# First norm of a two-layer diffusion backbone: the shift leaves the tile path, and six products get their bias from separate small matmuls

## What is computed

```python
def rmsnorm(x, g):
    y = xf * lax.rsqrt(jnp.mean(xf * xf, -1, keepdims=True) + NORM_EPS)
    return (y * g.astype(jnp.float32)).astype(x.dtype)

def modulate(h, g, shift, scale):
    return rmsnorm(h, g) * (1 + scale) + shift

def adaln_terms(s, w, b):
    return jnp.split(jax.nn.silu(s) @ w + b, N_MOD, -1)

def swiglu(x, w_up, w_down):
    gate, up = jnp.split(x @ w_up, 2, -1)
    return (jax.nn.silu(gate) * up) @ w_down
```

## Time and profile before

| | |
|---|---|
| three runs | 3075.9 us median (3070.89 to 3077.01) |
| span of the profiled execution | 3074.0 us |
| time before the fourth product, u1, starts on PE | 77.27 us |
| busy | PE 97%, DVE 52%, ACT 32%, POOL 32% |
| chain that ended last | PE 89%, of which the dense products 78% |

### The profile page before, as it was taken

The page is one execution under the profiler, slowest core; times in us unless marked ns, Lnnn a source line. Parts: engine busy times, 40 slices in busy tenths (PEclk is TensorE's granted clock), DMA queues, the critical chain, the costliest instruction groups (busy, mean ns, idle before and its releaser), DMA issues.

```text
span 3074.0 us, 45849 instructions
## 1 busy us (share of the span) xinstructions
PE 2973.5 (97%) x19023; PEld 2784.3 (91%) x19023; DVE 1600.5 (52%) x2437; ACT 983.4 (32%) x1700; POOL 996.1 (32%) x516
## 2 busy tenths in 40 slices
PE   6999999999999988999999999999999999999998
PEld 6999999999888876899999999999999877798997
DVE  6556666884646665576667783212123358431223
ACT  4211212343454456321121233212123247532222
POOL 5333333333332202233333332222222222344442
PEclk8999999999999999999999999999999999999999
DMA  4434444223320022234334331211211210132221
GB/s 190 141 114 135 122 141 138 89 85 120 115 68 15 8 87 77 89 112 149 126 130 142 121 117 64 69 56 63 68 61 50 81 42 2 63 101 92 90 96 70
DMA packets 126236, 284.25 MB, mean 92 GB/s; under 512 B 40222, under 2 KB 57550, under 8 KB 126030
## 3 DMA queue, kind: packets, MB, share of 16 engines
q1 hardware_dynamic: 123150, 274.86, 27.4%
q10 hardware_dynamic: 2880, 6.47, 0.5%
HBM read 269.68 MB, written 15.10 MB: 93 GB/s over the span
## 4 chain that ended last, share of the span: by engine, by line
PE 89%; DVE 5%; ACT 4%; issue 2%; POOL 0%; DMA 0%; ACTq 0%; SPq 0%; DVEq 0%; POOLq 0%
PE psum L1788 78%; PE psum L1962 2%; PE psum L2062 2%; PE psum L2050 1%; DVE o_acc L1618 1%; PE psum L2043 1%; PE psum L1947 1%; ACT prob_o L1269 1%; PE psum L2003 1%; DVE prob_o L1719 1%; PE psum L1982 1%; PE psum L1969 1%; PE psum L1992 0%; DVE probT_o L1731 0%; ACT cacc L1122 0%
## 5 line engine op out<-in xcount | busy, mean ns | idle before, releaser
L893 POOL TENSOR_TENSOR wl<-raw,wh 128x1024 fp32r<-128x1024 f32 (+1 forms) x329 | 838.2, 2548 | 1643.8 <-ACT wh L998 1642.6
L1788 PE MATMUL psum<-uh,wh 128*128 128x256 f32 (+5 forms) x2704 | 660.0, 325 | 24.7 <-DVE ul L1336 17.7
L1788 PE MATMUL psum<-ul,wh 128*128 128x256 f32 (+5 forms) x2704 | 658.6, 325 | 0.0
L1788 PE MATMUL psum<-uh,wl 128*128 128x256 f32 (+5 forms) x2704 | 658.5, 325 | 0.0
L1788 PE MATMUL psum<-ah,wh 128*128 128x386 f32 (+4 forms) x2192 | 596.4, 344 | 5.6 <-POOL wl L893 4.4
L1788 PE MATMUL psum<-ah,wl 128*128 128x386 f32 (+4 forms) x2192 | 591.3, 342 | 0.0
L1788 PE MATMUL psum<-al,wh 128*128 128x386 f32 (+4 forms) x2192 | 589.0, 341 | 0.0
L1788 PEld LDWEIGHTS psum<-uh,wh 128*128 128x128 f32 (+1 forms) x2704 | 450.7, 189 | 48.5 <-issue 21.5
L1540 DVE SCALAR_TENSOR_TENSOR ada_product<-ada_w,cb 128x1024 f32<-128x1024 f32 x256 | 478.1, 1868 | 5.1
L1788 PEld LDWEIGHTS psum<-uh,wl 128*128 128x128 f32 (+1 forms) x2704 | 450.6, 189 | 19.7
L1788 PEld LDWEIGHTS psum<-ul,wh 128*128 128x128 f32 (+1 forms) x2704 | 450.0, 189 | 19.8
(11 more groups left out here) (248 smaller groups left out, 2433.9 us busy)
## 6 DMA issues: line engine op xcount, KB each, us to landing
raw<-in_w SPq DMA_DIRECT2D x264, 512.0 KB, 3.6
ada_w<-in_ada_w SPq DMA_DIRECT2D x128, 512.0 KB, 3.6
raw<-in_w SPq DMA_DIRECT2D x64, 448.0 KB, 3.4
spill<-cacc ACTq DMA_DIRECT2D x16, 384.0 KB, 2.6
scale_w<-in_scale_w SPq DMA_DIRECT2D x8, 512.0 KB, 13.6
ada_start<-in_ada_w SPq DMA_DIRECT2D x8, 512.0 KB, 14.4
ada_w<-bias_final SPq DMA_DIRECT2D x16, 256.0 KB, 3.0
h<-in_xT SPq DMA_DIRECT2D x8, 384.0 KB, 13.8
```

The source lines that it names most:

```text
L893: nc.gpsimd.tensor_tensor(wl[n % SPLIT_SLOTS][:, 0:k * w], raw[n % RAW_SLOTS][:, 0:k * w], wh[n % SPLIT_SLOTS][:, 0:k * w].bitcast(f32), A ...
L1788: ins = nc.tensor.matmul(pair[0:w, lo:hi], wt[n % SPLIT_SLOTS][:, k * w:(k + 1) * w], xt[:, k, cols], start=first, stop=last)
```

## The change

- silu(c) is loaded as a row, broadcast by one DMA to all partitions (cb, 1 MB), and goes through SiLU on ACT (one 128x2048 instruction). The 16 spreading matmuls and the two copies are gone.
- The shift leaves the tile path: `start_scale`, gain, uh and ul stay per tile, all eight scales on PE (`PE_SCALES`). The 8 shift chunks, now two passes each, are made by DVE after the tiles: 2 chunks before the norm, 3 behind the scaling of the fused products, 3 behind that of u1.
- The first six products (`early`: g0, u0, g1, u1, g2, u2) run over 768 columns without the shift. A new item `bias` makes their biases: in the middle of u2 (k = 4, `BIAS_AT`) PE runs 6 x 8 x 2 = 96 matmuls of 4 or 2 moving columns over the weights of all six products, kept for that: the first three in buffers of their own (`start_wh`, `start_wl`), the next three in wh and wl, which so stay taken until then.
- Only then do SiLU and gating of these products run (ACT and DVE, behind `bias_copied`); DVE copies each bias into the two end columns.
- DVE makes the low parts of the first three weights and sums the squares; POOL has nothing to do in the start. Four of the eight shift chunks are loaded over the buffers of scales 0 to 3.
- In all norms the shift columns are written by one instruction per kind of token, not per tile.

```diff
+EARLY = 6
+PE_SCALES = (0, 1, 2, 3, 4, 5, 6, 7)
+CHUNKS_BEFORE_NORM, CHUNKS_BEFORE_FOURTH = 2, 5
+BIAS_AT = 4
...
+            load_start(2)
+            sp.dma_start(cb[:, :, :].rearrange("p v d -> p (v d)"), a["c_rows"].to_broadcast([P, 2 * D])).then_inc(c_rows_loaded, 16)
...
+            sp.wait_ge(start_gain, 4)
+            for k in range(4, KD):
+                load_ada_start(k)
...
-                    if n >= SPLIT_SLOTS:
-
-                        act.wait_ge(product_done, number[slots[n - SPLIT_SLOTS][0]] + 1)
...
+                    if n >= FUSED + SPLIT_SLOTS:
+                        y = slots[n - SPLIT_SLOTS][0]
+                        act.wait_ge(product_done, number[("bias",) if y in early[FUSED:-1] else y] + 1)
...
+                elif x[0] == "bias":
+                    act.wait_ge(start_shift, 1)
+                    for v in range(2):
+                        nc.scalar.activation(shift_x[:, :, 1 - v], mod[:, 0, 0, :, v], ACT.Copy)
+                    shift_high(0, uh)
+                    split_up_to(EARLY + 1)
+                    for y in early[:-1]:
+                        finish_product(y)
...
+                if x in early:
+                    nc.vector.tensor_tensor(t[:, 1:1 + T], bank[:, AT:AT + T], rstd[:, 1:1 + T], ALU.mult).then_inc(scaled, 1)
...
-                ada_chunk(ada_order[k])
+                for n in ((0,), (1, 2))[k] if k < 2 else ():
+                    low_split(n)
                 late_low(norm_items[0], k)
-                start_shifts(k)
-                dve.wait_ge(shift_hi, k + 1)
-                shift_low(0, k).then_inc(shift_lo, 1)
-            dve.wait_ge(c_rows_copied[1], 1)
+                if k:
+                    add_square(0, k - 1)
+            add_square(0, KD - 1)
+            for c in ada_order[:CHUNKS_BEFORE_NORM]:
+                ada_chunk(c)
...
+                elif x == early[FUSED]:
+                    scale_product(x)
+                    for c in ada_order[CHUNKS_BEFORE_FOURTH:ADA_FIRST]:
+                        ada_chunk(c)
+                    start_shifts()
...
+            def early_biases():
+
+                pe.wait_ge(scaled, scaled_no[early[FUSED]] + 1)
+                pe.wait_ge(shift_lo, 1)
+                for y in early:
+                    n, bank = slot_of[y], bias_columns(y)
+                    for k in range(KD):
+                        nc.tensor.matmul(bank, high_weight(n)[:, P * k:P * k + P], shift_x[:, k, :], start=k == 0, stop=False)
+                        ins = nc.tensor.matmul(bank[:, 0:2], low_weight(n)[:, P * k:P * k + P], shift_x[:, k, 0:2],
+                                               start=False, stop=k == KD - 1)
+                ins.then_inc(product_done, 1)
...
-                    pe.wait_ge(ident_loaded, 16)
-                    for v in range(2):
-                        for q in range(KD):
-                            ins = nc.tensor.matmul(c_rows(v)[:, P * q:P * q + P], c_cols[:, q, v:v + 1].to_broadcast([P, P]), ident[:, :],
-                                                   start=True, stop=True)
-                    ins.then_inc(c_rows_made, 1)
...
                         pe.wait_ge(late_lo, k + 1)
-                        pe.wait_ge(shift_lo, k + 1)
...
+                    if x == early[-1]:
+                        ready = lambda k: early_biases() if k == BIAS_AT else None
```

More of the change, by code:

```diff
@@ L72, in over @@
             plan.setdefault(chosen[len(chosen) * c // len(chunks)], []).append(chunk)
-    at = [i for i, x in enumerate(items) if x[0] in ("gate", "up", "down") and x[1:3] == (0, 0)][FUSED:]
+    at = [i for i, x in enumerate(items) if x[0] in ("gate", "up", "down") and x[1:3] == (0, 0)][EARLY - 1:]
     n = next(k for k, i in enumerate(at) if items[i][0] == "down")
@@ L84, in schedule @@
     late = lambda m, products, n=1: products[:n] + [("norm", m)] + products[n:]
-    s = [("start",)] + late(0, ffn_products(0, 0), FUSED)
+    s = insert_before([("start",)] + late(0, ffn_products(0, 0), FUSED), ffn_products(0, 0)[EARLY - 1], [("bias",)])
     if mixers:
@@ L235, in build @@
     late_proj = {l: [x for x in late_items if x[0] == "proj" and x[1] == l] for l in range(DEPTH)}
-    fused = ahead[0]
+    fused, early = ahead[0], [x for x in late_items if norm_of(x) == 0][:EARLY]
     with ExitStack() as ctx:
@@ L429, in released @@
                 return [(start_gain, KD)]
+            if kind == "bias":
+                return [(bias_copied, 2 * EARLY)]
             if kind in RESIDUAL:
@@ L475, in build @@
                 place[x] = (4, 1)
+            elif kind == "bias":
+                place[x] = (7, 1)
             elif kind in ("vt", "start"):
@@ L498, in start_bank, with bias_columns, high_weight, low_weight @@
         def start_bank(k):
-            return banks_of(("start",))[:, 512 * (k % 2):512 * (k % 2) + 2]
-        def c_rows(v):
-            return psum[:, D * v:D * v + D]
+            b = PE_SCALES.index(k) % 2
+            return banks_of(("start",))[:, 512 * b:512 * b + 2]
+        def bias_columns(x):
+            return banks_of(("bias",))[:, 4 * early.index(x):4 * early.index(x) + 4]
+        def high_weight(n):
+            return start_wh[n] if n < FUSED else wh[n % SPLIT_SLOTS]
+        def low_weight(n):
+            return start_wl[n] if n < FUSED else wl[n % SPLIT_SLOTS]
         def segs_of(x):
@@ L1059, in late_high @@
                     act.wait_ge(mod_ready, mod_terms(x, 0, 1))
-                    for k in range(KD):
-                        ins = shift_high(m, k, high)
-                    ins.then_inc(shift_hi, 1)
+                    shift_high(m, high)
                 for v, (lo, hi) in enumerate((LAT, CTX)):
@@ L1536, in ada_chunk @@
                     w, product = ada_w[n % ADA_BUFS], ada_product
-                for v in range(2 if n >= ADA_FIRST else 1):
+                if n == 0:
+                    dve.wait_ge(c_rows_ready, 1)
+                for v in range(2):
                     if on_dve(n) + v:
@@ L1593, in _ @@
                         for y in ahead[x[1]]:
-                            finish_product(y)
+                            if m:
+                                finish_product(y)
+                            else:
+                                scale_product(y)
+                    if m == 0:
+                        for c in ada_order[CHUNKS_BEFORE_NORM:CHUNKS_BEFORE_FOURTH]:
+                            ada_chunk(c)
+                elif x[0] == "bias":
+                    shift_low(0)
+                    for y in early[:FUSED + 1]:
+                        copy_bias(y)
+                    for y in early[1:-1]:
+                        finish_product(y)
+                elif x == early[FUSED]:
+                    scale_product(x)
+                    for c in ada_order[CHUNKS_BEFORE_FOURTH:ADA_FIRST]:
+                        ada_chunk(c)
+                    start_shifts()
+                elif x in early[FUSED + 1:-1]:
+                    pass
                 elif x[0] == "spread":
@@ L1785, in dense_step @@
                 K, w = slots[n][1:]
-                for wt, xt, first, last in ((wh, xh, k == 0, False), (wh, xl, False, False), (wl, xh, False, k == K - 1)):
+                high, low = high_weight(n), low_weight(n)
+                for wt, xt, first, last in ((high, xh, k == 0, False), (high, xl, False, False), (low, xh, False, k == K - 1)):
                     for lo, hi, cols in moving(x):
-                        ins = nc.tensor.matmul(pair[0:w, lo:hi], wt[n % SPLIT_SLOTS][:, k * w:(k + 1) * w],
+                        ins = nc.tensor.matmul(pair[0:w, lo:hi], wt[:, k * w:(k + 1) * w],
                                                xt[:, k, cols], start=first, stop=last)
```

174 lines of the change are left out of this document (87 added, 87 removed).

## The result

The changed kernel takes 3084.4 us (median of 7 runs, 3081.2 to 3086.3) against 3075.9 us: 1.0032 times the time before, with a 95% interval of 1.0021 to 1.0042. It is slower, by about 10 us, and the forecast was 3086 us.

What follows compares the result with a forecast made beforehand. PE, at 97% of the span, was taken as the bound. A gain of 23.4 us up to u1 against 33.2 us lost behind it put u3 9.9 us later: forecast 3086 us, range 3070 to 3091.

Steps and rivals of the forecast that it cites:

- The tile path: Scales and fused tiles before u1: PE sets the pace, u1 starts at 53.9 instead of 77.27, 23.4 us gained.
- rival 4: Tile loop: two-column rows between tiles lower the clock, some 30 us more, time above 3105 us; chance 0.03.
- The shift's date: DVE's passes, reciprocal and scalings after the last tile: shift ready at 84.8 us.
- Where PE waits before it: PE between u1 and the bias rows: g2's wait costs 3.0 us, the wait for the shift 6.7 us.
- The block: The 96 bias matmuls in the middle of u2: half speed, 0.22 us a row, 21.1 us, ending at 105.9.
- Rival 1: Bias rows at the lower weight-load price of 0.17: 16.3 us, time 3081; part of the forecast's range, no separate chance.
- rival 2: Bias rows: PE, busy without a gap, wins the full clock back; 12.3 us, time 3077, no change; chance 0.24.
- Behind the block: From the bias rows to u3: slow half of u2, late gating chain of 15.2 us, u3 at 121.1 instead of 111.25.
- Rival 3: DVE's chain: shift ready at 78, PE keeps full clock, bias rows cost 10.2 us, time 3068; chance 0.13.

Runs made afterwards that it cites:

- e7: Changed kernel with six DVE shift passes spread singly over gaps in tiles 4 to 7, none left before the reciprocal: 3078.2 us.
- e2: Changed kernel with 26 unused 384-column matmuls filling PE's wait for the shift before the bias rows: 3081.0 us.
- e6: Changed kernel with the shift columns repeated 64 times, so bias rows have 256 and 128 moving columns: 3080.6 us.
- e10: e8 without its 14 filler matmuls: 3071.6 us.
- e8: Changed kernel with e7's spread passes, 14 filler matmuls, bias rows of 256/128 columns, and u3's weight also split before the late gating: 3068.5 us.
- e12: e8 without the further split of u3's weight before the late gating: 3069.9 us.
- e11: e8 with bias rows of 4 and 2 moving columns instead of 256 and 128, filler kept: 3074.5 us.
- e5: Changed kernel with the shift columns repeated 16 times, so bias rows have 64 and 32 moving columns: 3086.1 us.
- e9: Changed kernel with its sixteen DVE shift passes cut to 8 of 1024 columns and 12 bias rows instead of 96: 3057.4 us.

## Why the prediction was right, point by point

- **The tile path** (u1 at 53.9, 23.4 us won): measured 53.73 and 23.5. The steps hold one by one: second scale at half speed (9.84, 3.57 us), first fused tile at half speed (5.1 us from 13.27 to 18.37), then six times scale and tile by some 4.97 us (18.37, 23.28, ... 43.13). One row was misnamed: what PE goes on with at 15 in the kernel before is the second scale, not the first. The two-column rows between the tiles did not lower the clock, so rival 4 was rightly small.
- **The shift's date** (84.8): the bias rows start at 85.14. DVE was free at 49.67 (predicted 49.6); two passes were slowed as predicted, by 2.0 us each (2.4 in the sum). The reciprocal began at 58.71 instead of 59.4; u2's split did not fall beside the reciprocal, and cost 1.3 of the 2.4 named for that case.
- **Where PE waits before it**: the sum was right (9.7 predicted for g2 and the shift together, 10.2 measured), but not its parts. I gave g2 3.0 and the shift 6.7. Measured: g2 2.5, then 1.8 because g2 ran its first rows at half speed behind the 2.25 us wait, 1.2 for u2's own bank, which waits for DVE between the passes, and 4.7 at the shift. The 1.8 and the 1.2 were missing from the prediction. They cost nothing, because all of it ends at the same date on DVE: what PE loses earlier it no longer waits there. e7 shows both sides: without the waits for banks, the wait for the shift is still 3.3.
- **The block** (21.1, by 0.22 a row; it "carries 11 us alone"): 20.05, by 0.213 a row, and the first rows at 0.11 because the clock falls a little into the block, not before it. The row that decided was the first scale: two-column rows that stay at half speed without a gap. That reading has a weak spot that the prediction does not name. The half speed was read from the spacing of the rows; the granted clock (the third number from the end) in the same stretch of the kernel before reads 1.00:

```profile
6.00:9.40 3.40, 3.34 (x16) 1.00 1.06 409
```

  The spacing is the better witness: in the changed kernel the first fused tile, right behind the two scales, takes 5.10 us with the column at 1.00 as well, as long as the tile at 26.46 before, where the column says 0.50. The column reads 1.00 over this start in all thirteen traces, so it seems to miss the slow start; why is open. In the changed kernel two such scales, 32 rows over 7.1 us, stay at half speed. Rival 1's lower price, 0.17, shows nowhere as a spacing that lasts.
- **The block doesn't win the clock back** (rival 2, 0.24): right, and e2 shows more than I had argued, since the clock also fell from full within such rows. Here the Trainium skill was weighed (TensorE: Matmul & The Clock Gate, section on the HAM clock gate), whose rule is that the gate follows how busy the engine has lately been. With 256/128 columns (e6, e10) the trace agrees. With 4/2 and 64/32 columns it doesn't, if busy means what the profile's busy column says: 5.00 of 5.00 us, and 0.50. Nor does the page's fixed rate for a weight load (section LDWEIGHTS) hold at both clocks: the rows are 0.11 us apart at the full clock, as an estimate from it says (10.2 us for 96), and 0.213 at half.
- **Behind the block**: slow half 1.8 predicted, 2.1 measured; u3's own wait 0.6 predicted, 1.6 measured. What sets the date is the chain of late gating, from the block's end to u3: 121.66 - 105.19 = 16.5 us instead of 15.2. Its instructions took about what the prediction gave them; left out were the 0.1 to 0.3 us between the end of one and the start of the next on another engine, which sum to some 1.2 in the changed kernel's trace.
- **Rival 3** (0.13; "decides from a shift at about 79.5 on, and only with the full clock"): both conditions were met in turn. e7 has the shift at 78.46 without the clock, and is 0.12% above before. e8 and e12 have both, and run at 3068.5 and 3069.9 us, where the rival said 3068. But they have it only with the wider rows. With the rows of the change itself e11 meets both conditions at the start of the block (79.25, a wait of 0.54, full clock), loses the clock after 14 rows and runs at 3074.5, no change. So with these rows an early shift alone did not bring the rival's block of 10.2 us.

The errors at u3 are +0.3 for the shift's date, -1.0 for the block and +1.3 for the chain behind it: together +0.5 us (10.4 against 9.9), and the runs say 9.8. That the last two nearly cancel is luck; the terms themselves were each within 1.3 us.

## What to carry to other kernels

Work that is taken off a path and put elsewhere in one block costs its whole length if the engine of that path has to run it, so price the block by the rate at which the engine will then be running, not by its best rate. Look in the trace for the nearest row of the same shape, and see at which clock it went on. Here small matmuls behind a wait ran at the lower clock to the end, and more moving columns behind the same weight load were free. Look also at what starts only when the block is done: here 16.5 us of late gating, in which PE had 12.75 us of work. When a chain on another engine sets a date, waits before that date need not be told apart: only the date counts.

## What the runs showed of the hardware

- 96 matmuls with 4 and 2 moving columns, back to back, stayed at the granted clock of 0.50 (1.2 GHz) for 20 us. Entered at 1.00 (2.4 GHz), they fell to 0.50 without a gap, after 41 rows in e2 and 14 in e11 (one trace each). 64 and 32 columns behaved alike (e5). With 256 and 128 they won the full clock back after 6.4 us (e6) and 3.4 us (e10) at half speed, and kept it when they had it (e8, e12).
- A pair of bias rows, each behind a 128x128 weight load, takes 0.22 us at the full clock and 0.43 at half, whether they have 4 and 2 or 256 and 128 moving columns.
- The full clock was lost behind waits of PE of 2.25 us (g2), 2.6 (u3 in e10), 3.3 (e7, e10), 3.5 to 3.6 (u3 in e6, e9 and e12) and 4.4 (the bias rows of the changed kernel), and also 0.8 us behind one of 1.9 (u3 in e5). It was kept behind those of 0.4 to 1.75 us (the tiles of the kernel before, the block in e8, u1, u2, u3), but also behind the one of 2.6 at u3 in e8.
- A pass of DVE with two inputs from on-chip memory took 2.5 to 3.4 us beside a split on POOL, 1.22 alone. The Trainium skill has it (SBUF — State Buffer, section "Who interferes with whom"): the two engines share a port pair, and the second to come waits for the whole instruction of the first. The durations here agree: 1.22 and what is left of a 2.4 us split when the pass's turn comes (2.51 at 66.30, with the split begun at 65.35).
